# Expert and router weights laid out with eight neighbouring channels on a partition

## What is computed

```python
D_MODEL, SEQ, N_EXPERTS, D_EXPERT = 1024, 1024, 32, 512
t = rmsnorm(x, moe_norm)                      # (1024 tokens, 1024 channels)
g_prob = softmax(t @ w_group + b_group)       # 4 groups, the best one is taken
e_logits = t @ w_router + b_router            # 8 experts in a group, the best two
# tokens sorted by expert, in blocks of 128 rows, each block of one expert e:
xb = t[toks]                                  # (128, 1024)
hid = silu(xb @ w_gate[e]) * (xb @ w_up[e])   # (128, 512)
y = (hid @ w_down[e]) * gates                 # (128, 1024), added back to the tokens
```

## Time and profile before

| | |
|---|---|
| median of three runs | 3510.33 us |
| the profiled execution | 3513.74 us, span 3511.9 us |
| TensorE matmul busy | 2972.1 us, 85% of the span |
| VectorE busy | 1971.5 us, 56% |
| ScalarE busy | 1518.9 us, 43% |
| POOL busy | 633.2 us, 18% |
| SyncE's DMA queue (q1) | 263408 packets, 513.73 MB, 40.8% of 16 engines' span |

### The profile page before, as it was taken

One profiled execution on the slowest core, in us unless ns is written; L12 is line 12 of the kernel. 1 busy time (PEld: TensorE's weight loads), 2 busy tenths in 40 slices (PEclk: granted clock), 3 DMA queues, 4 the chain that ended last, 5 costly groups with the idle time before them and its releaser, 6 DMA issues. The chain is left out here.

```text
span 3511.9 us, 42490 instructions
## 1 busy us (share of the span) xinstructions
PE 2972.1 (85%) x13528; PEld 2263.7 (64%) x13528; DVE 1971.5 (56%) x2493; ACT 1518.9 (43%) x1704; POOL 633.2 (18%) x501
## 2 busy tenths in 40 slices
PE   3988888999759999995798999677699669999992
PEld 2433366765448777784787788466588557777771
DVE  3212454550258888886410455576644368888885
ACT  2001343440128888883311233232301148888882
POOL 1000000000011111111110445487600011111102
PEclk9999898999859999997599999887899679999996
DMA  4211410100329999996131232333220359999994
GB/s 174 78 56 35 128 35 28 36 18 0 122 91 386 397 399 396 398 397 237 41 107 53 82 93 92 129 106 106 72 96 31 121 210 395 396 399 398 397 392 167
DMA packets 302645, 640.45 MB, mean 182 GB/s; under 512 B 21616, under 2 KB 80112, under 8 KB 302448
## 3 DMA queue, kind: packets, MB, share of 16 engines
q1 hardware_dynamic: 263408, 513.73, 40.8%
q10 hardware_dynamic: 23040, 67.12, 4.8%
q0 software_dynamic: 16128, 58.73, 4.5%
HBM read 545.14 MB, written 94.37 MB: 182 GB/s over the span
## 5 line engine op out<-in xcount | busy, mean ns | idle before, releaser
L1884 DVE TENSOR_TENSOR moe_w_low<-moes_raw,moe_w_high 128x2048 fp32r<-128x2048 f32 x384 | 864.1, 2284 | 184.9 <-ACT moe_w_high L1811 184.9
L1811 ACT ACTIVATE moe_w_high<-moes_raw 128x2048 fp32r<-128x2048 f32 x384 | 720.4, 1920 | 98.6 <-PEq L162 67.1
L1705 POOL COPY moe_pick<-moes_tokens 128x1 int32 (+1 forms) x64 | 62.9, 983 | 1778.2 <-PE moe_px L1730 856.8
L186 PE MATMUL moe_py<-moe_w_high,moe_h_high 128*128 128x512 f32 x512 | 210.6, 411 | 0.0
L186 PE MATMUL moe_pg<-moe_w_high,moe_x_high 128*128 128x512 f32 x512 | 207.3, 405 | 0.0
L186 PE MATMUL moe_pu<-moe_w_high,moe_x_high 128*128 128x512 f32 x512 | 205.6, 402 | 0.0
L188 PE MATMUL moe_pg<-moe_w_high,moe_x_low 128*128 128x512 f32 x512 | 204.6, 400 | 0.0
L187 PE MATMUL moe_pg<-moe_w_low,moe_x_high 128*128 128x512 f32 x512 | 204.5, 399 | 0.0
L188 PE MATMUL moe_pu<-moe_w_high,moe_x_low 128*128 128x512 f32 x512 | 203.1, 397 | 0.0
L188 PE MATMUL moe_py<-moe_w_high,moe_h_low 128*128 128x512 f32 x512 | 203.1, 397 | 0.0
L187 PE MATMUL moe_pu<-moe_w_low,moe_x_high 128*128 128x512 f32 x512 | 202.9, 396 | 0.0
(11 more groups left out here) (367 smaller groups left out, 6308.2 us busy)
## 6 DMA issues: line engine op xcount, KB each, us to landing
moes_raw<-in_w_gate SPq DMA_DIRECT2D x128, 1024.0 KB, 7.4
moes_raw<-in_w_up SPq DMA_DIRECT2D x128, 1024.0 KB, 8.6
moes_raw<-in_w_down SPq DMA_DIRECT2D x128, 1024.0 KB, 7.3
Y<-moe_y ACTq DMA_DIRECT2D x64, 512.0 KB, 6.5
conv_raw<-in_w_in_ssd SPq DMA_DIRECT2D x24, 512.0 KB, 4.9
XC<-conv_c ACTq DMA_DIRECT2D x24, 512.0 KB, 2.9
Y<-B POOLq DMA_DIRECT2D x16, 512.0 KB, 12.2
HN<-norm_m_hn SPq DMA_DIRECT2D x16, 512.0 KB, 2.6
```

The costliest lines, as they stand in the source:

```text
L186: nc.tensor.matmul(out, lh, rh, start=start, stop=False)
L1705: nc.gpsimd.tensor_copy(pick[a][:, :], M.tokens[:, bass.ds(b, 1)]).then_inc(picked[a], 1)
L1811: nc.scalar.activation(wh[c % SPLIT_SLOTS][:, :], M.raw[j][:, :], ACT.Copy).then_inc(w_high, 1)
L1884: nc.vector.tensor_tensor(wl[j][:, :], M.raw[c % RAW_SLOTS][:, :], bits(wh[j][:, :]), ALU.subtract).then_inc(w_low, 1)
```

## The change

The view of the expert weights and of the router's weights goes from `(k p)` to `(p k)`: partition p now holds channels 8p to 8p+7 (4p to 4p+3 of `hid` for the down product). A piece is then one run of 8 KB on each partition, for all three matrices; the router's weights are one run of 1152 bytes on a partition, where they were eight of 144. So that the other factor comes in the same order, VectorE writes `hn` and `hid` permuted: column j of the tile goes to block j mod 8 (j mod 4 for `hid`). The instruction reads in order and writes with a step of 128 values, 512 bytes, from one value to the next. `HN` is stored and gathered in the permuted order. Nothing else is changed; the transposes read their 128 columns as before.

```diff
@@ expert_stage, hidden(i, a), VectorE
-                nc.vector.tensor_tensor(hid[:, :], sg[:, :], pu[:, :], ALU.mult).then_inc(hid_ok, 1)
+                nc.vector.tensor_tensor(hid[:, :].rearrange("p (k q) -> p q k", k=FK), sg[:, :].rearrange("p (q k) -> p q k", k=FK),
+                                        pu[:, :].rearrange("p (q k) -> p q k", k=FK), ALU.mult).then_inc(hid_ok, 1)
@@ moe_norm_stage, VectorE
-                nc.vector.scalar_tensor_tensor(out=hn[t % 2][:, :], in0=K.X[:, t, :], scalar=rstd[:, t:t + 1], in1=gf[:, :],
+                nc.vector.scalar_tensor_tensor(out=hn[t % 2][:, :].rearrange("p (k q) -> p q k", k=ND),
+                                               in0=K.X[:, t, :].rearrange("p (q k) -> p q k", k=ND), scalar=rstd[:, t:t + 1],
+                                               in1=gf[:, :].rearrange("p (q k) -> p q k", k=ND),
                                                op0=ALU.mult, op1=ALU.mult).then_inc(rows, 1)
@@ moe_layer
-        source = {kind: A[f"w_{kind}"][layer].rearrange("e (k p) n -> e p k n", p=P) for kind in ("gate", "up", "down")}
+        source = {kind: A[f"w_{kind}"][layer].rearrange("e (p k) n -> e p k n", p=P) for kind in ("gate", "up", "down")}
@@ moe_layer, first_weights(sp)
-            sp.dma_start(M.wr[:, :, :], A["w_route"][layer].rearrange("(k p) n -> p k n", p=P)).then_inc(M.wr_loaded, 16)
+            sp.dma_start(M.wr[:, :, :], A["w_route"][layer].rearrange("(p k) n -> p k n", p=P)).then_inc(M.wr_loaded, 16)
```

## The result

| kernel | median, us | lowest to highest | runs | the profiled span |
|---|---|---|---|---|
| before | 3510.33 | 3509.54 to 3513.15 | 5 | 3511.9 |
| changed | 3527.63 | 3524.43 to 3532.89 | 5 | 3525.8 |

The ratio is 1.0048, with an interval of 1.0034 to 1.0063. The change costs 17 us; I had forecast a gain of 9. The number lies beside that of rival A.

A forecast was written before the change was run, and what follows sets the result against it. TensorE was taken to set the pace, with loads keeping up. Terms -10.8 + 0 + 1 = -9.8 us against the median of 3510.33 gave 3501 us; the forecast's own range was 3496 to 3506, over all cases 3491 to 3533.

The forecast's parts named there:

- rival A: Rival: the permuted write costs about as much as the stepped read, TensorE waits longer for `hid`; 3529 us, chance 0.30.
- What bounds the kernel: Expert stages: TensorE sets the pace at 36.94 us a round, idle 0.37 us for `hid`; d more on `hid` adds 2d.
- Steady loads: Weight loads in the expert stages: larger runs should be faster, but no engine waits for a piece; gain in time nothing.
- First weights: End of the norm stage: SyncE's six issues take 0.5 us each, the router starts 5.4 us sooner; -10.8 us, two layers.
- bounds of 8 and 12.8: Range given for the gain from quicker issues at the norm stage's end, both layers: between -8 and -12.8 us.
- The stepped writes: VectorE's permuted writes of `hid` and `hn`: cost between 0 and 28 us, taken as 0.
- s: Extra ns for each value that VectorE writes with the large step; bounded by 0 and 0.69, taken as 0.
- first sign of being wrong: In the expert stage: a `hid` above 0.8 us, with a wait for it above 0.6 us.
- formula around s: Cost of the permuted writes at s ns more a value: 30.7s us in the rounds, 10.2s in the norm, 41s together.
- my own sum: Total over both layers: -10.8 for quicker issues, 0 for permuted writes, +1 for gathers; -9.8 us.
- Gathers: Second gather before round 0: may land later beside larger weight runs; +0.5 us a layer, +1 in all.
- The clock: TensorE's clock at the router: its small matmuls held 1.2 GHz for 27.5 us in both layers; nothing counted for starting earlier.

## Why the prediction was wrong, step by step

**What bounds the kernel: right.** TensorE sets the pace, its one regular hole is `hid`, and what lengthens `hid` by d lengthens the round by 2d. Measured: 0.33 and 0.27 us more from the start of either `hid` to the next instruction's, and 0.64 us more for the round.

**Steady loads: right.** DMA share down from 1.04 to 1.00, no gain in time; the half with 8 KB runs for gate and up keeps its rounds at 36.9 us.

**First weights: right, slightly too large.** 4.6 and 5.2 us for the two layers instead of 5.4 each; an issue takes 0.49 to 0.67 us, not 0.5. (My bounds of 8 and 12.8 don't follow from the rows that I named: 0.58 and 0.37 us an issue give 9.9 and 12.4. Measured are 9.8.) The explanation by runs waiting (4096 before, 896 after) is borne out by the two halves: with gate and up in 8 KB runs the six issues (four gate, two up) are quick, with only down changed they are as slow as before (router's waits 7.4 against 18.5 us in all, 18.0 in the trace of before). Moving three of them out of the stage takes the same wait away without the layout.

**The stepped writes: this step failed.** I had bounded s between 0 and 0.69 ns for a value and taken 0, on a judgement that a write need not cost what the stepped read of the earlier trace rows cost. By the length of the instruction it is 0.68 measured alone at this step, 0.77 for `hid` (above my upper bound) and 0.69 for `hn`, about the price of the stepped read each time. The first sign of being wrong that I had named came true with it: `hid` above 0.8 us and a wait for it above 0.6.

The formula around s was sound. What VectorE loses is a little less than the length, because the next instruction starts before one has ended: 0.30 us a `hid` on average from start to start. With that, 30 x 2 x 0.30 = 18.0 us stand against 18.2 measured between the stages' first and last `hid`; with s = 0.69 it would be 21.2. For the norm 10.2 x 0.69 = 7.0 stand against 6.5. With the upper bound put in, my own sum would have been 3529, and 3527.63 was measured. That it is so close is partly luck: 3.5 us too much on the stepped writes stand against 2.5 us behind the stages' last `hid` that I had not counted, and 1.0 too much gain on the first weights. The nearest row was the only evidence in the trace; I set against it a judgement that no row supported, and took the end of the range instead of the row.

The rule of the Trainium skill in "Advanced Engine Details and Errata", section "SBUF Cachelines" (lines of 16 bytes, a penalty for an access that goes to another line each time), agrees with the runs: on VectorE a step of 2 values of 4 bytes is free (693 ns against 692), a step of 4 values is not (1073), and larger steps cost no more. The size is measured here, 0.66 to 0.76 ns a value on VectorE, and writes pay it as reads do, on ScalarE too.

**Gathers: right in sign.** +1.5 us in all, where I had taken +1. **The clock: right for the router.** Its matmuls ran at half clock (27.49 us) as before, in both layers. I had not looked at the first products of the expert stage, where layer 1 gained 0.9 us.

**The chances.** A had 0.30, with the one stepped row of the trace for it and only that judgement against it. That was too little.

What stays open: no run moved `keep_h` by itself, so that it opens the gap in the next round is read from the traces and not tested; and 1.7 us behind the stages' last `hid` are not placed.

## What to carry to other kernels

If an operand is rearranged to make a transfer cheaper, price the rearrangement at the engine that performs it, and look where that instruction stands: 0.4 us twice a round, before a deadline, was worth 18 us here, and the same 0.4 us elsewhere in the order next to nothing (0.04 us a round). Where transfers are hidden, cheaper transfers give only what waits for their issue, and that wait may be removed more simply by issuing fewer of them before a barrier. When a step has no row of its own, take the nearest row's value, unless another row speaks against it. And when moving an instruction off one deadline, follow its engine's unbroken work to the next deadline before counting the gain.

## What the runs showed of the hardware

A VectorE product of 128 x 512 values takes 692 ns with steps of 1 or 2 values, and 1029 to 1080 ns with steps of 4 to 128, whether the step is on the output or on one input. A copy on ScalarE takes 630 ns at a step of 1, 673 at 2, and 1083 to 1128 at 4 to 128. SyncE's issue of a load of 1 MB behind its like took 0.49 to 0.67 us where it had 128 runs, and 1.4 us on average (8.36 us for six) where it had 512.
